# Gate and up products of two feed-forward layers: high weights times both halves of the activations in one product of 512 columns

## The chip, the cores and the metric

The program runs on one core of a Trainium2 chip. A core has TensorE (matrix products, with a queue of weight loads of its own), VectorE, ScalarE, GpSimd, SyncE (which here only starts transfers) and 16 DMA engines. The metric is the device time of one execution in microseconds, lower is better; the figure quoted for a kernel is the median of its runs.

## The reference, cut to what matters

The reference is a model of two blocks on 256 tokens of 1024 features. The first block has two layers, and each ends with a gated feed-forward. The change concerns the first two products of it, `h @ w1` (gate) and `h @ w3` (up):

```
D_FF = 2816
def swiglu(h, w1, w3, w2):
    return (jax.nn.silu(h @ w1) * (h @ w3)) @ w2

for i in range(2):                                    # the first block
    ...                                               # mixer: attention and convolution, or a Fourier transform
    x = x + g2 * swiglu(rmsnorm(x, norm2_g[i]) * (1 + sc2) + sh2, ffn_w1[i], ffn_w3[i], ffn_w2[i])
x = second_block(x, ...)                              # attention, recurrence, 32 experts, a last norm
```

The scales `sc2`, shifts and gates of a layer come from a product of a condition vector with a large matrix (`ada_w`), which the kernel computes alongside on VectorE.

## The kernel before, in words

The work is written out by hand for each engine: every engine runs its own list in order, and semaphores tie the lists together. Nothing schedules it at build time.

**High and low parts.** TensorE multiplies in a float32 form that keeps fewer bits. To keep float32 accuracy every operand is split: `wh` is the rounded weight tile and `wl` is what is left, `ah` and `al` are the same for the activations. A product is then three matmuls into one sum: `wh*ah`, `wh*al` and `wl*ah`. ScalarE makes the high part (a copy that rounds), VectorE the low part (a subtraction).

**A feed-forward layer** (`ffn(l)`, l = 0 or 1, one in each layer) walks over 22 tiles f of 128 hidden features. For each tile:
- TensorE `gate_up(f)`: for gate and for up (`half`), 8 steps j over the 1024 input features, three matmuls of 256 columns (the tokens) each: 48 matmuls, lines 808 to 810. Gate and up of one tile share one PSUM bank, `ps[f % 2]`.
- ScalarE `sigmoid(f)` reads gate (line 1338), then `ffn_hi` makes the high part of the gate and up weights of tile f + 2 (line 1317, 2048 columns), `mul_hi` the high part of the hidden tile (line 1342), `down_hi` that of the down weights of tile f + 1 (line 1348).
- VectorE `mul(f)`: gate times sigmoid (line 1910), times up (line 1912). `mul_lo` makes the low part of the hidden tile (line 1917), `wide_lo` that of the gate and up weights of tile f + 2 (line 1740, two instructions), `down_lo` that of the down weights of tile f + 1 (line 1922). Two `ada_step` instructions per tile (lines 1624 and 1625, 1024 columns) sum the product of the condition vector; each waits for a transfer into `araw`.
- TensorE `down(f)`: 24 matmuls of 256 columns, lines 821 to 823, once `mul_lo(f)` and `down_lo(f)` are there.

TensorE's order is gate_up(0), gate_up(1), down(0), then gate_up(f + 2), down(f + 1) and so on, so that VectorE and ScalarE have the time of the next gate_up to finish a tile. Tiles 0 to 19 run in a loop of five rounds of four tiles (`u` = 0 to 3), tiles 20 and 21 after it. SyncE starts, per tile, one transfer of 1 MB (gate and up weights), one of 0.5 MB (down weights) and two of 0.5 MB for `araw`; each waits until the tile that it overwrites has been used.

**After the last tile** VectorE does two ada steps (`ada(base_n + 42)` and `+ 43`), which release SyncE to fetch the last block of weights that ScalarE has to split (line 1175) before it squares x for the next norm (line 1185); TensorE sums the squares (line 611).

Of the kernel before, what the change touches and what calls it, by code (L numbers as in the profile page):

```python
# [15 lines left out]
P = 128  # L16
# [117 lines left out]
def build(nc, xT_d, xc_d, vec_d, con_d, cone_d, tab_d, ada_d, blk_d, uq_d, uk_d, ffna_d, ffnb_d, rga_d, rgx_d, rout_d,  # L134
# [5 lines left out]
    with ctx:  # L140
        def sb(name, shape, dt=F32, stack=ctx):
            return stack.enter_context(nc.sbuf_tensor(name, shape, dt))
# [33 lines left out]
        def q_scale(i):  # L176
# [8 lines left out]
        wl = sb("wl", [P, 6144], F32R, early)  # L185
        ah = sb("ah", [P, DJ * 2 * T], F32R, early)
        al = sb("al", [P, DJ * 2 * T], F32R, early)
        cone = sb("cone", [P, NE_], F32, early)
        ah3 = ah[:, :].rearrange("p (j t) -> p j t", j=DJ)
        al3 = al[:, :].rearrange("p (j t) -> p j t", j=DJ)  # L190
        ph = ExitStack()
# [144 lines left out]
        s_lg, s_tk, s_tke, s_mask, s_cum, s_route, s_ht, s_htok, s_flag = [sem(n) for n in (  # L336
            "logits", "top_values", "top_exp", "chosen", "slot_counts", "routed", "h_turned", "h_tokens", "overflow_known")]
        s_order, s_pick, s_gpp, s_gpc = [sem(n) for n in ("experts_ranked", "ranks_set", "places_product", "places_copied")]
# [8 lines left out]
        s_last = sem("last_output_copied")  # L347
        s_ot, s_fy = sem("out_turned"), sem("final_chunk")

# [208 lines left out]
        def _(pe):  # L558
# [239 lines left out]
            def ffn(l):  # L798
                def gate_up(f, fv, fresh=None):
                    wait(pe, s_flo, f + (l * NF + 1))  # L800
                    wait(pe, s_fm, f + (l * NF - 1))
                    for half in range(2):
                        for j in range(DJ):
                            if fresh is not None:
                                pe.wait_ge(s_hl, DJ * fresh + j + 1)
                            w0 = (fv % 2) * FA + half * D + j * P
                            o = ps[fv % 2][:, half * T:(half + 1) * T]
                            mm(o, wh[:, w0:w0 + P], ah3[:, j, 0:T], start=(j == 0), stop=False)  # L808
                            mm(o, wh[:, w0:w0 + P], al3[:, j, 0:T], start=False, stop=False)  # L809
                            last = mm(o, wl[:, w0:w0 + P], ah3[:, j, 0:T], start=False, stop=(j == DJ - 1))  # L810
                    last.then_inc(s_fgu, 1)
# [344 lines left out]
            for j in range(DJ):  # L1156
                mm(out_tile(j), ymo[:, j * P:(j + 1) * P], stt[:, (NU - 1) % 3, :], start=False, stop=True,
                   skip_group_check=True).then_inc(s_ot, 1)
            norm_sums(6)
# [3 lines left out]
        def _(act):  # L1163
# [171 lines left out]
            def ffn(l):  # L1335
                def sigmoid(f, slot):
                    wait(act, s_fgu, f + (l * NF + 1))
                    A(sg[:, slot, :], ps[slot][:, 0:T], ACT.Sigmoid).then_inc(s_fsig, 1)

# [270 lines left out]
        def _(dve):  # L1610
# [294 lines left out]
            def ffn(l, g_gate):  # L1905
                base_n, base_g = 48 + 48 * l, 6 + 6 * l

                def mul(f, slot):
                    wait(dve, s_fsig, f + (l * NF + 1))
                    TTn(sg[:, slot, :], ps[slot][:, 0:T], sg[:, slot, :], ALU.mult).then_inc(s_ft, 1)  # L1910
                    wait(dve, s_ft, f + (l * NF + 1))
                    TTn(mm_[:, slot, :], ps[slot][:, T:2 * T], sg[:, slot, :], ALU.mult).then_inc(s_fm, 1)

# [12 lines left out]
                with dve.Fori(0, (NF - 2) // 4) as i:  # L1926
# [4 lines left out]
                    for u in range(4):  # L1931
                        mul(f0 + u, u % 2)
                        for j in (2 * u, 2 * u + 1):
                            dve.wait_ge(s_araw[j % 2], loaded + 16 * (j // 2))
                            if j > 0:
                                dve.wait_ge(s_ada, n0 + j)
                            ada_step(accl[:, bass.ds(g0, AG)], araw[:, j % 2, :], csil[:, j:j + 1] if l == 0 else V("c2", j), j
                                     ).then_inc(s_ada, 1)
                            if j % 2 == 0:
                                mul_lo(f0 + u, u % 2)  # L1940
                                wide_lo(l, f0 + (2 + u), u)
                        down_lo(f0 + (u + 1), (u + 1) % 2)
# [451 lines left out]
```

## Time and profile before

| | us |
|---|---|
| median of 3 runs (1874.78, 1878.18, 1877.59) | 1877.59 |
| the profiled execution, whole | 1875.9 |
| its span, first to last instruction | 1874.1 |
| TensorE busy in the span | 1682.5 (90%) |
| VectorE busy | 808.7 (43%) |
| ScalarE busy | 436.9 (23%) |

The two feed-forward stages lie at about 270 to 462 us and 548 to 741 us of the span. After 1000 us the experts run. A row of the profile names the line of the kernel, the engine, the operation, and `out<-in` by the program's names. Shares over the whole span say little about a stage, since the stages have different limits.

### The profile page before, as it was taken

To read this page: it belongs to the slowest core of one execution; us is meant where nothing else is said; L and a number is where in the kernel's file an instruction comes from. 1 tells how busy PE (TensorE), PEld (TensorE's weight loads), DVE (VectorE), ACT (ScalarE), POOL (GpSimd) and SP (SyncE) were. 2 spreads that over 40 slices of the span, in tenths; PEclk is the share of its full clock that TensorE was granted. 3 is DMA by queue.
4 is the path that set the end of the run, shared out by engine and by line. 5 is a ranking of instruction groups with operands and counts; after the bars stand their busy time and mean duration, and the time that the engine had idled before them with its cause. 6 is when DMAs were issued, how large, how long until landed. Compare 5 with 4: busy or idle time off the path is not lost.

```text
span 1874.1 us, 24283 instructions
## 1 busy us (share of the span) xinstructions
PE 1682.5 (90%) x9444; PEld 1066.2 (57%) x9444; DVE 808.7 (43%) x1263; ACT 436.9 (23%) x679; POOL 157.1 (8%) x75
## 2 busy tenths in 40 slices
PE   5989799999899998876899999999987988799875
PEld 2863489998589998866633444334322433344222
DVE  5766568877348877575322222212211212122021
ACT  3324644443334443354200000000000000000001
POOL 1632010000210001452000000000000000000000
PEclk8998899999899999798899999999998999899988
DMA  8723448886328886334799999999999999999994
GB/s 323 248 79 142 150 157 304 305 302 240 144 102 305 310 298 230 130 146 150 300 392 421 421 421 422 421 421 421 421 422 421 421 422 422 420 410 422 421 421 196
DMA packets 100606, 586.61 MB, mean 313 GB/s; under 512 B 12224, under 2 KB 13504, under 8 KB 45152
## 3 DMA queue, kind: packets, MB, share of 16 engines
q1 hardware_dynamic: 100512, 585.35, 79.8%
q8 instruction: 59, 0.97, 0.2%
q14 instruction: 35, 0.29, 0.0%
HBM read 584.26 MB, written 1.05 MB: 312 GB/s over the span
## 4 chain that ended last, share of the span: by engine, by line
PE 74%; DMA 11%; DVE 8%; SPq 3%; ACT 2%; issue 1%; POOL 0%; DVEq 0%; ACTq 0%
PE psum L1047 22%; PE psum L1063 10%; PE psum L808 5%; PE psum L809 5%; PE psum L810 5%; DMA mraw<-dn_dram 5%; SPq L401 3%; PE psum L1023 3%; DMA mraw<-gu_dram 2%; PE psum L626 2%; PE psum L1076 2%; PE psum L627 2%; PE psum L628 2%; PE psum L823 2%; PE psum L822 2%; PE psum L821 2%
## 5 line engine op out<-in xcount | busy, mean ns | idle before, releaser
L1047 PE MATMUL psum<-mraw,xsat 128*64 128x512 f32 (+2 forms) x1648 | 416.5, 646 | 38.3 <-DMA mraw<-gu_dram 25.2
L1047 PEld LDWEIGHTS psum<-mraw,xsat 128*64 128x64 f32 (+2 forms) x1648 | 137.7, 144 | 272.4 <-issue 271.4
L1063 PE MATMUL psum<-mraw,xsat 128*64 128x512 f32 (+2 forms) x848 | 204.6, 620 | 13.4 <-DMA mraw<-dn_dram 10.7
L808 PE MATMUL psum<-ah,wh 128*128 128x256 f32 x704 | 202.5, 288 | 7.2 <-DVE al L1684 7.1
L1569 POOL TENSOR_TENSOR wl<-raw,wh 128x1024 fp32r<-128x1024 f32 x56 | 147.2, 2647 | 719.2 <-ACT wh L1175 689.9
L809 PE MATMUL psum<-al,wh 128*128 128x256 f32 x704 | 200.8, 285 | 0.0
L810 PE MATMUL psum<-ah,wl 128*128 128x256 f32 x704 | 200.7, 285 | 0.0
L626 PE MATMUL psum<-ah,wh 128*128 128x256 f32 (+1 forms) x440 | 136.1, 309 | 29.5 <-DVE al L2104 8.4
L1047 PE MATMUL psum<-mlast,xsat 128*64 128x512 f32 (+2 forms) x400 | 145.6, 648 | 17.0 <-DMA mraw<-gu_dram 17.0
L808 PEld LDWEIGHTS psum<-ah,wh 128*128 128x128 f32 x704 | 136.5, 194 | 8.5 <-issue 7.6
L1063 PEld LDWEIGHTS psum<-mraw,xsat 128*64 128x64 f32 (+2 forms) x848 | 68.0, 140 | 122.2 <-issue 120.3
L809 PEld LDWEIGHTS psum<-al,wh 128*128 128x128 f32 x704 | 136.9, 194 | 0.0
L810 PEld LDWEIGHTS psum<-ah,wl 128*128 128x128 f32 x704 | 136.8, 194 | 0.0
L2212 DVE TENSOR_TENSOR oacc<-psum,oacc 128x512 f32<-128x512 f32 x60 | 38.6, 686 | 220.9 <-PE psum L1076 220.9
L627 PE MATMUL psum<-al,wh 128*128 128x256 f32 (+1 forms) x440 | 132.6, 301 | 0.0
L628 PE MATMUL psum<-ah,wl 128*128 128x256 f32 (+1 forms) x440 | 132.3, 301 | 0.0
L1535 ACT ACTIVATE xsat<-psum 128x512 f32<-128x512 f32 x16 | 9.6, 599 | 436.2 <-PE psum L1096 436.2
L626 PEld LDWEIGHTS psum<-ah,wh 128*128 128x128 f32 x440 | 90.1, 205 | 36.1 <-issue 14.3
L1740 DVE TENSOR_TENSOR wl<-raw,wh 128x1024 fp32r<-128x1024 f32 x88 | 103.7, 1220 | 0.0
L821 PE MATMUL psum<-mh,wh 128*128 128x256 f32 x352 | 99.6, 283 | 0.0
L822 PE MATMUL psum<-ml,wh 128*128 128x256 f32 x352 | 99.6, 283 | 0.0
L823 PE MATMUL psum<-mh,wl 128*128 128x256 f32 x352 | 99.6, 283 | 0.0
(355 smaller groups left out, 2382.9 us busy)
## 6 DMA issues: line engine op xcount, KB each, us to landing
mraw<-gu_dram SPq DMA_DIRECT2D x206, 1024.0 KB, 19.8
mraw<-dn_dram SPq DMA_DIRECT2D x106, 1024.0 KB, 25.3
araw<-ada_dram SPq DMA_DIRECT2D x128, 512.0 KB, 4.7
mlast<-gu_dram SPq DMA_DIRECT2D x50, 1024.0 KB, 20.9
raw<-ffa_dram SPq DMA_DIRECT2D x44, 1024.0 KB, 7.7
raw<-blk_dram SPq DMA_DIRECT2D x56, 512.0 KB, 4.3
raw<-ffb_dram SPq DMA_DIRECT2D x44, 512.0 KB, 5.8
mlast<-dn_dram SPq DMA_DIRECT2D x22, 1024.0 KB, 26.1
```

Of the source, the lines that this page charges most:

```text
L626: mm(o, wh[:, w], ah3[:, j, 0:width], start=(j == 0), stop=False)
L627: mm(o, wh[:, w], al3[:, j, 0:width], start=False, stop=False)
L628: last = mm(o, wl[:, w], ah3[:, j, 0:width], start=False, stop=(j == DJ - 1))
L808: mm(o, wh[:, w0:w0 + P], ah3[:, j, 0:T], start=(j == 0), stop=False)
L809: mm(o, wh[:, w0:w0 + P], al3[:, j, 0:T], start=False, stop=False)
L810: last = mm(o, wl[:, w0:w0 + P], ah3[:, j, 0:T], start=False, stop=(j == DJ - 1))
L821: mm(o, wh[:, w0:w0 + P], a, start=first and j % 2 == 0, stop=False, skip_group_check=True)
L822: mm(o, wh[:, w0:w0 + P], b_, start=False, stop=False, skip_group_check=True)
L823: last = mm(o, wl[:, w0:w0 + P], a, start=False, stop=end, skip_group_check=True)
L1047: last = mm(ps[4 + n][a * w:(a + 1) * w, :], xs[:, k * P + a * w:k * P + (a + 1) * w], slots[slot][:, i * 2 * D + n * 512:i * 2 * D + (n + ...
L1063: last = mm(ps[n][a * w:(a + 1) * w, :], at[:, k * P + a * w:k * P + (a + 1) * w], slots[slot][:, i * D + n * 512:i * D + (n + 1) * 512], ...
L1569: sub = lambda o, a, b: nc.gpsimd.tensor_tensor(o, a, b.bitcast(F32), ALU.subtract)
```

## The change

Three things change together.

1. The two activation halves lie in one tensor, `ahl[:, 0]` high and `ahl[:, 1]` low. `gate_up` multiplies `wh` by both at once: one matmul of 512 columns fills a whole bank, columns 0 to 255 with `wh*ah`, columns 256 to 511 with `wh*al`. A second matmul of 256 columns adds `wl*ah` to the first half. Gate and up take a bank each, so four banks are used in place of two.
2. The two halves of a bank have to be added. ScalarE copies the right halves of gate and up to SBUF (into `rt` and `rstd`, which are free here), VectorE adds them to the left halves in PSUM (`halves`), and only then ScalarE takes the sigmoid.
3. VectorE's order within a tile changes: `halves`, the first ada step, `mul`, `wide_lo`, the second ada step, `mul_lo`, `down_lo`. Before it was `mul`, the first ada step, `mul_lo`, `wide_lo`, the second ada step, `down_lo`.

TensorE also waits for `s_mod` before gate_up(1), since bank 2 held a result of the condition vector's product; and one semaphore of the last stage is merged into another.

```diff
@@ gate_up, TensorE
-                            o = ps[fv % 2][:, half * T:(half + 1) * T]
-                            mm(o, wh[:, w0:w0 + P], ah3[:, j, 0:T], start=(j == 0), stop=False)
-                            mm(o, wh[:, w0:w0 + P], al3[:, j, 0:T], start=False, stop=False)
-                            last = mm(o, wl[:, w0:w0 + P], ah3[:, j, 0:T], start=False, stop=(j == DJ - 1))
+                            bank = ps[2 * (fv % 2) + half]
+                            if j < DJ - 1:
+                                mm(bank[:, :], wh[:, w0:w0 + P], ahl4[:, :, j, 0:T], start=(j == 0), stop=False)
+                                mm(bank[:, 0:T], wl[:, w0:w0 + P], ah3[:, j, 0:T], start=False, stop=False)
+                            else:
+                                mm(bank[:, 0:T], wl[:, w0:w0 + P], ah3[:, j, 0:T], start=False, stop=False)
+                                last = mm(bank[:, :], wh[:, w0:w0 + P], ahl4[:, :, j, 0:T], start=False, stop=True)
@@ ffn, TensorE
                 gate_up(0, 0, fresh=1 + l)
+                pe.wait_ge(s_mod, 6 + 6 * l)
                 gate_up(1, 1)
@@ sigmoid, ScalarE
                     wait(act, s_fgu, f + (l * NF + 1))
-                    A(sg[:, slot, :], ps[slot][:, 0:T], ACT.Sigmoid).then_inc(s_fsig, 1)
+                    A(rt[:, T:2 * T], ps[2 * slot][:, T:2 * T], ACT.Copy)
+                    A(rstd[:, T:2 * T], ps[2 * slot + 1][:, T:2 * T], ACT.Copy).then_inc(s_fsig, 1)
+                    wait(act, s_fsum, f + (l * NF + 1))
+                    A(sg[:, slot, :], ps[2 * slot][:, 0:T], ACT.Sigmoid).then_inc(s_fsig, 1)
@@ ffn, VectorE
+                def halves(f, slot):
+                    wait(dve, s_fsig, f * 2 + (l * NF * 2 + 1))
+                    gate, up = ps[2 * slot][:, 0:T], ps[2 * slot + 1][:, 0:T]
+                    TTn(gate, gate, rt[:, T:2 * T], ALU.add).then_inc(s_fsum, 1)
+                    TTn(up, up, rstd[:, T:2 * T], ALU.add)
...
                     for u in range(4):
-                        mul(f0 + u, u % 2)
+                        halves(f0 + u, u % 2)
                         for j in (2 * u, 2 * u + 1):
...
                             if j % 2 == 0:
+                                mul(f0 + u, u % 2)
+                                wide_lo(l, f0 + (2 + u), u)
+                            else:
                                 mul_lo(f0 + u, u % 2)
-                                wide_lo(l, f0 + (2 + u), u)
                         down_lo(f0 + (u + 1), (u + 1) % 2)
+                halves(NF - 2, 0)
                 mul(NF - 2, 0)
...
+                halves(NF - 1, 1)
                 mul(NF - 1, 1)
```

On VectorE, the first tile of a round of the loop (u = 0). Before; `accl` is the sum of the condition vector's product, `wl` from `raw,wh` a low part of weights, `ml` the low part of the hidden tile:

```order
L1910 TENSOR_TENSOR sg<-psum,sg 128x256 [waits ffn_sigmoid]
L1912 TENSOR_TENSOR mm_<-psum,sg 128x256 [waits ffn_gate]
...
L1624 TENSOR_SCALAR accl<-araw,csil 128x1024
L1917 TENSOR_TENSOR ml<-mm_,mh 128x256 [waits ffn_mul_hi]
...
L1740 TENSOR_TENSOR wl<-raw,wh 128x1024 [waits ffn_hi]
L1740 TENSOR_TENSOR wl<-raw,wh 128x1024
...
L1922 TENSOR_TENSOR wl<-raw,wh 128x1024 [waits ffn_down_hi]
```

The same place on VectorE with the change (its own line numbers):

```order
L1924 TENSOR_TENSOR psum<-psum,rt 128x256 [waits ffn_sigmoid]
L1925 TENSOR_TENSOR psum<-psum,rstd 128x256
...
L1631 TENSOR_SCALAR accl<-araw,csil 128x1024
...
L1917 TENSOR_TENSOR sg<-psum,sg 128x256 [waits ffn_sigmoid]
...
L1919 TENSOR_TENSOR mm_<-psum,sg 128x256 [waits ffn_gate]
...
L1747 TENSOR_TENSOR wl<-raw,wh 128x1024 [waits ffn_hi]
L1747 TENSOR_TENSOR wl<-raw,wh 128x1024
...
L1632 SCALAR_TENSOR_TENSOR accl<-araw,csil,accl 128x1024 [waits ada_acc]
L1930 TENSOR_TENSOR ml<-mm_,mh 128x256 [waits ffn_mul_hi]
...
L1935 TENSOR_TENSOR wl<-raw,wh 128x1024 [waits ffn_down_hi]
```

The two additions come first, and the row that writes `ml` has moved from behind the first ada step to behind `wide_lo` and the second ada step.

On ScalarE, the head of a round of the loop. Before:

```order
L1338 ACT_TABLE_LOAD
L1338 ACTIVATE sg<-psum 128x256 [waits ffn_gate_up]
L1315 ISA
L1317 ACTIVATE wh<-raw 128x2048 [waits wide_loaded0]
L1342 ACTIVATE mh<-mm_ 128x256 [waits ffn_mul]
```

And with the change:

```order
L1342 ACT_TABLE_LOAD
L1342 ACTIVATE rt<-psum 128x256 [waits ffn_gate_up]
L1343 ACTIVATE rstd<-psum 128x256
L1345 ACT_TABLE_LOAD
L1345 ACTIVATE sg<-psum 128x256 [waits ffn_halves_added]
L1319 ISA
L1321 ACTIVATE wh<-raw 128x2048 [waits wide_loaded0]
L1349 ACTIVATE mh<-mm_ 128x256 [waits ffn_mul]
```

Two copies stand ahead of the sigmoid, and a second load of ScalarE's function table now stands between them and the sigmoid. It does so only here, once a round; the other three tiles of a round and tiles 20 and 21 have none.

## Rows read from the trace of the kernel before

**Rows 1.** By window: us, busy PE, PEld, DVE, ACT, POOL; clock; DMA share, GB/s.

```profile
275.00:460.00 185.00, 185.00 (x1544) 185.00 (x1544) 146.30 (x172) 80.58 (x91) 0.76 (x1) 1.00 0.83 289
```

**Rows 2.** Timeline, TensorE, gate_up: start us, length us, engine, line.

```profile
350.06 0.28 PE L808 MATMUL psum<-ah,wh 128*128 128x256 f32 x1
...
355.46 0.28 PE L808 MATMUL psum<-ah,wh 128*128 128x256 f32 x1
```

**Rows 3.** Timeline, TensorE, products of 512 columns in the first stage.

```profile
64.07 0.40 PE L626 MATMUL psum<-ah,wh 128*128 128x512 f32 x1
...
73.60 0.39 PE L626 MATMUL psum<-ah,wh 128*128 128x512 f32 x1
```

**Rows 4.** Timeline, VectorE, one tile of feed-forward 0 and the next one's start.

```profile
353.19 0.42 DVE L1910 TENSOR_TENSOR sg<-psum,sg 128x256 f32<-128x256 f32 x1 [1.51 <-ACT sg L1338]
...
354.00 1.27 DVE L1625 SCALAR_TENSOR_TENSOR accl<-araw,csil,accl 128x1024 f32 x1
355.30 0.42 DVE L1917 TENSOR_TENSOR ml<-mm_,mh 128x256 fp32r<-128x256 f32 x1
355.64 2.36 DVE L1740 TENSOR_TENSOR wl<-raw,wh 128x1024 fp32r<-128x1024 f32 x2
357.91 1.28 DVE L1625 SCALAR_TENSOR_TENSOR accl<-araw,csil,accl 128x1024 f32 x1
359.11 1.22 DVE L1922 TENSOR_TENSOR wl<-raw,wh 128x1024 fp32r<-128x1024 f32 x1
361.83 0.42 DVE L1910 TENSOR_TENSOR sg<-psum,sg 128x256 f32<-128x256 f32 x1 [1.51 <-ACT sg L1338]
```

**Rows 5.** Timeline, ScalarE, the same tile.

```profile
352.78 0.38 ACT L1338 ACTIVATE sg<-psum 128x256 f32<-128x256 f32 x1 [4.64 <-PE psum L810]
353.06 1.90 ACT L1317 ACTIVATE wh<-raw 128x2048 fp32r<-128x2048 f32 x1
```

**Rows 6.** Timeline, ScalarE, tiles 0 and 1 of feed-forward 0.

```profile
274.58 1.28 ACT L1338 ACT_TABLE_LOAD   x1
277.90 0.38 ACT L1338 ACTIVATE sg<-psum 128x256 f32<-128x256 f32 x1 [2.03 <-PE psum L810]
...
283.66 0.39 ACT L1338 ACTIVATE sg<-psum 128x256 f32<-128x256 f32 x1 [2.32 <-PE psum L810]
```

**Rows 7.** Timeline, VectorE, tiles 0 to 2 of feed-forward 0.

```profile
279.11 0.74 DVE L1624 TENSOR_SCALAR accl<-araw,csil 128x1024 f32 x1
280.42 0.42 DVE L1917 TENSOR_TENSOR ml<-mm_,mh 128x256 fp32r<-128x256 f32 x1 [0.56 <-ACT mh L1342]
...
285.36 0.42 DVE L1910 TENSOR_TENSOR sg<-psum,sg 128x256 f32<-128x256 f32 x1
...
295.56 1.29 DVE L1625 SCALAR_TENSOR_TENSOR accl<-araw,csil,accl 128x1024 f32 x1 [1.96 <-DMA araw<-ada_dram]
```

**Rows 8.** Timeline, TensorE, idle gaps of 1.6 to 3 us.

```profile
269.65 0.36 PE L808 MATMUL psum<-ah,wh 128*128 128x256 f32 x1 [2.55 <-DVE al L1684]
...
844.89 0.66 PE L915 MATMUL psum<-con,p 128*128 128x128 f32 x4 [2.20 <-DVE p L2047]
...
853.67 3.41 PE L946 MATMUL psum<-q,con 128*128 128x256 f32 x8 [2.22 <-ACT q L1463]
```

**Rows 9.** TensorE in the 4 us behind three such gaps: us, busy, clock.

```profile
270.00:274.00 4.00, 3.89 (x18) 0.57 0.00 0
845.00:849.00 4.00, 2.27 (x13) 1.00 0.00 0
854.00:858.00 4.00, 4.00 (x12) 0.57 0.00 0
```

**Rows 10.** Chain of waits, end of feed-forward 0: start us, length us, what.

```profile
456.46 0.39 ACT sg L1338
...
459.97 3.25 DVE acc L1625
...
463.67 4.94 DMA raw<-blk_dram
```

More of the change, by code:

```diff
@@ L185, in build @@
         wl = sb("wl", [P, 6144], F32R, early)
-        ah = sb("ah", [P, DJ * 2 * T], F32R, early)
-        al = sb("al", [P, DJ * 2 * T], F32R, early)
+        ahl = sb("ahl", [P, 2, DJ * 2 * T], F32R, early)
         cone = sb("cone", [P, NE_], F32, early)
-        ah3 = ah[:, :].rearrange("p (j t) -> p j t", j=DJ)
-        al3 = al[:, :].rearrange("p (j t) -> p j t", j=DJ)
+        ahl4 = ahl[:, :, :].rearrange("p a (j t) -> p a j t", j=DJ)
+        ah3, al3 = ahl4[:, 0], ahl4[:, 1]
         ph = ExitStack()
@@ L329, in build @@
         s_th, s_lruo = sem("lru_tanh"), sem("lru_out")
+        s_fsum = sem("ffn_halves_added")
         s_zero = sem("pads_cleared")
@@ L336, in build @@
         s_lg, s_tk, s_tke, s_mask, s_cum, s_route, s_ht, s_htok, s_flag = [sem(n) for n in (
-            "logits", "top_values", "top_exp", "chosen", "slot_counts", "routed", "h_turned", "h_tokens", "overflow_known")]
+            "logits", "top_values", "top_exp", "chosen", "slot_counts", "routed", "tokens_and_output_turned", "h_tokens", "overflow_known")]
         s_order, s_pick, s_gpp, s_gpc = [sem(n) for n in ("experts_ranked", "ranks_set", "places_product", "places_copied")]
@@ L347, in build @@
         s_last = sem("last_output_copied")
-        s_ot, s_fy = sem("out_turned"), sem("final_chunk")
+        s_fy = sem("final_chunk")
         def out_tile(j):
@@ L1157, in _ @@
                 mm(out_tile(j), ymo[:, j * P:(j + 1) * P], stt[:, (NU - 1) % 3, :], start=False, stop=True,
-                   skip_group_check=True).then_inc(s_ot, 1)
+                   skip_group_check=True).then_inc(s_ht, 1)
             norm_sums(6)
@@ L1908, in mul @@
                 def mul(f, slot):
-                    wait(dve, s_fsig, f + (l * NF + 1))
-                    TTn(sg[:, slot, :], ps[slot][:, 0:T], sg[:, slot, :], ALU.mult).then_inc(s_ft, 1)
+                    wait(dve, s_fsig, f * 2 + (l * NF * 2 + 2))
+                    TTn(sg[:, slot, :], ps[2 * slot][:, 0:T], sg[:, slot, :], ALU.mult).then_inc(s_ft, 1)
                     wait(dve, s_ft, f + (l * NF + 1))
-                    TTn(mm_[:, slot, :], ps[slot][:, T:2 * T], sg[:, slot, :], ALU.mult).then_inc(s_fm, 1)
+                    TTn(mm_[:, slot, :], ps[2 * slot + 1][:, 0:T], sg[:, slot, :], ALU.mult).then_inc(s_fm, 1)
+                def halves(f, slot):
[3 more added lines that the diff above has]
+                    TTn(up, up, rstd[:, T:2 * T], ALU.add)
                 def mul_lo(f, slot):
@@ L2271, in _ @@
             for j in range(DJ):
-                dve.wait_ge(s_ot, j + 1)
+                dve.wait_ge(s_ht, 4 + j + 1)
                 STT(x[:, j, :], out_tile(j), m_col(17, j), x[:, j, :], ALU.mult, ALU.add).then_inc(s_x, 1)
```

## The prediction

> **What bounds the kernel now.** I read the busy times by window first, since the change touches two stages only. Over 275 to 460 us, feed-forward 0, TensorE is busy for all of the 185.00 us at a granted clock of 1.00 (2.4 GHz); VectorE works 146.30 us of it and the DMA engines 83% [rows 1]. So TensorE sets the pace of the stage, and I read the timelines of the engines next, to see how much room the others have. The second layer looks alike.
>
> TensorE's pace: from the L808 row at 350.06 to the one at 355.46 there are 45 matmuls, so one of 256 columns takes 0.120 us [rows 2]. A tile has 48 in gate_up and 24 in down, 72 x 0.120 = 8.64 us, which is just the distance of the two L1910 rows, 353.19 and 361.83 [rows 4]. In each tile VectorE sits idle for 1.51 us before L1910, waiting for ScalarE's sigmoid, and ScalarE 4.64 us for TensorE [rows 4, 5]. At the ends of a stage another thing decides, the chain of waits [rows 10], which I come to below.
>
> **TensorE, the gain.** The columns do not change: 512 + 256 is 3 x 256. What goes is one matmul and one weight load out of three. How much is that? In the first stage the kernel has products of 512 columns: from 64.07 to 73.60 there are 42 of them, 0.227 us each [rows 3], where two of 256 take 0.240 us. The saving is 0.013 us per pair, 16 pairs per tile, 0.21 us, and gate_up falls from 5.76 to 5.55 us, the tile from 8.64 to 8.43. The first gate_up of a stage is fed by VectorE and partly at the low clock, so I count half of it, 0.1. Two stages: 2 x (21 x 0.21 + 0.1) = 9.0 us, if every tile stays at TensorE's pace.
>
> The Trainium skill, "TensorE: Matmul & The Clock Gate", section "Wait — 56ns, not 53.3ns?", gives a fixed cost of about 2.5 ns per matmul at the high clock; by that, 704 matmuls fewer would save 1.8 us, not 9.0, and the change would come out 7 us later. The trace disagrees: 0.120 us is 13 ns over 256 columns at 2.4 GHz, and the wide rows carry the same 13 ns once [rows 2, 3].
>
> **VectorE and ScalarE in an ordinary tile.** Let z be the moment when ScalarE starts on a tile. Before, the copy from PSUM takes 0.28 us to the next start and 0.38 to its end, the copy of 2048 columns 1.90, and VectorE starts at z + 0.41 [rows 4, 5]. VectorE's pieces from start to start: two multiplications 0.81, first ada step 1.30, `mul_lo` 0.34, `wide_lo` 2.27, ada step 1.20, `down_lo` about 1.2 [rows 4]. With the change: copies to 0.66; additions from 0.69 to 1.39 (I take 0.35 each, a row of the same kind and size; no row shows VectorE writing PSUM); ada step to 2.6; sigmoid done at 1.5, hidden; `mul` to 3.4; the wide copy of ScalarE is done at 3.3, hidden; `wide_lo` to 5.7; ada step to 6.9; `mul_lo` done at 7.3; `down_lo` to 8.4. TensorE wants `mul_lo` at z + 8.43 (down of the tile before, 2.88, and a gate_up, 5.55), and VectorE is wanted again at 8.43 + 0.69 = 9.12. Both are met: margins 1.1 and 0.7 us. Bounds of an addition: 0.28 (ScalarE's copy of the size) to 0.74 (a 1024-column step of VectorE, the next dearer row [rows 7]). At the upper end two additions cost 0.8 us more and eat the margins without passing them by more than 0.1.
>
> In a tile with u = 0, the order of ScalarE now has a table load of 1.28 us [rows 6] between the copies and the sigmoid. Copies to 0.66, load to 1.96, sigmoid to 2.36, wide copy 2.26 to 4.16. VectorE's ada step is the short one here (0.74, [rows 7]), but `wide_lo` has to wait until 4.18; it ends at 6.45, the ada step at 7.65, `mul_lo` at 8.07. TensorE wants it at 8.43. Hidden, with a margin of only 0.36.
>
> **The start of a stage, a new stall.** TensorE's order there is gate_up(0), gate_up(1), down(0): only one gate_up lies between the end of tile 0's gate_up and its down, not a down and a gate_up. So TensorE wants `mul_lo(0)` at z + 5.55. Before, that row began at 280.42, z being 277.90: z + 2.5, early by 3 us [rows 6, 7]. Now it is a tile with u = 0, done at 8.09 as above. TensorE stands still for 8.09 - 5.55 = 2.54 us, in each of the two stages: 5.1 us. Nothing behind it on TensorE's queue can fill in.
>
> A second stall follows in tile 2. VectorE left tile 0 at 285.36, z + 7.46, and now leaves at z + 9.14, and `down_lo(1)` releases SyncE, behind which the loads of tile 4 and of `araw` queue. The ada step of tile 2 already waited 1.96 us for its transfer, until z + 17.66 [rows 7]. I move the landing by the same 1.7 to 19.3; this step now stands ahead of `mul`, so `mul_lo(2)` follows 5.9 us later (1.2 + 0.8 + 2.3 + 1.2 + 0.4), at 25.2. TensorE wants it at 8.09 + 2.88 + 5.55 + 8.43 = 24.95. Cost 0.3 us, in feed-forward 0. Together 5.4.
>
> **The end of a stage, a longer chain.** The chain that ends the stage goes from the last gate_up through ScalarE's sigmoid at 456.46, VectorE, an ada step of 3.25 us (slowed beside GpSimd), then SyncE and a transfer of 4.94 us that ScalarE must split before the next norm [rows 10]. Tile 21 has no table load, but the chain gets longer: the multiplication began 0.41 after z; now copies 0.66, addition 0.42, sigmoid 0.39 and three hand-overs of 0.03 make 1.57. That is 1.16 per stage, 2.3 us. TensorE's down(21) also waits 0.4, but this lies beside the chain.
>
> Sum without the clock: -9.0 + 5.4 + 2.3 = -1.3 us. The profiled execution took 1875.9 (span 1874.1 and 1.8 around it), 1.7 below the median; applied to the median, 1877.6 - 1.3 = 1876.3.
>
> **The clock.** The new stall is a gap of 2.5 us in the middle of dense work. What did such gaps do? After 2.55 us before 269.65 the granted clock was 0.57 over the next 4 us, that is, it fell to 1.2 GHz for most of them, which cost 0.43 x 4 = 1.7 us. After 2.22 us before 853.67 it was 0.57 too. After 2.20 us before 844.89 it stayed at 1.00 [rows 8, 9]. So a fall is likelier than not. During it TensorE is slower, VectorE catches up, and the second stall of 0.3 goes. With a fall in both stages: -1.3 + 3.4 - 0.3 = +1.8, and 1877.6 + 1.8 = 1879.4; with one, about 1877.9. The wait on `s_mod` costs nothing: it is released at the stage's start, beside gate_up(0). I predict 1879.0.
>
> **The rivals.**
> - *Only the gain comes* (16%): start and end do not cost, because VectorE gets through tile 0 before TensorE needs it, or the transfer behind the chain lands when it did. For it: TensorE sets the pace over 185 us. Against it: the order of `mul_lo` behind `wide_lo`. Time 1877.6 - 9.0 = 1868.6; with half of the cost 1872.
> - *The wide product saves nothing* (12%, slower): its moving operand is in two pieces 16 KB apart, and no row shows such a one at 512 columns. If the step from one piece to the next costs the 13 ns that a matmul's start costs, the gain is nil, and stalls, chain and clock stay: +5.4 + 2.3 + 1 to 3 = about 1887. It decides from 8 ns per product on. (The 2.5 ns of the Trainium skill, "TensorE: Matmul & The Clock Gate", would put the time near here as well, at 1886; rows 2 and 3 leave it hardly a chance.)
> - *The low clock lasts longer* (13%, slower): over 6 to 7 us per gap, 3.3 us each: 1876.3 + 6.6 = 1882.9.
> - *VectorE becomes the pace* (5%, slower): its tile has 7.0 us beside the two additions, so it passes TensorE's 8.43 from 0.72 us per addition on and the old 8.64 from 0.82 on. At 1.0 us it would be 9.0 us per tile, 38 x 0.36 = +14, and 1893.
>
> **How the numbers follow.** The forecast (clock falls once or twice) has 54%, own range 1875 to 1882. What can be told from no change is 0.2%, 3.8 us: 1873.8 to 1881.4. Faster: the first rival and a little of the forecast's lower side, 18%. Slower: the last three rivals, all but a few parts of the long fall, 28%. Within: 54%. The range reaches from the first rival's edge to the unsaving product, 1869 to 1887.
>
> **What would show it.** Right: L809 and L813 of 512 columns 0.227 us apart from the next start; tiles 8.43 us apart; TensorE idle about 2.5 us before the first down row of each stage, waiting for VectorE's `ml`; `mul_lo` 8.1 us after z in tile 0; a second table load between copy and sigmoid in ten tiles; the granted clock at 0.5 behind the gap; the ada steps of tile 21 about 1.2 us later after z. Wrong: tiles at 8.64 or more, or idle time of TensorE in the middle of a stage (the margins were too thin); no gap at the start (then faster by 5); additions over 0.7 us.

## The result, and the profile after

The changed kernel takes 1879.08 us (median of 20 runs, 1873.79 to 1886.41), the kernel before 1874.80 in the runs beside it (20 runs, 1871.31 to 1878.18). The ratio is 1.0022 with a 95% interval of 1.0013 to 1.0031: 4.1 us slower, 2.4 to 5.8. The profiled execution took 1873.79 us, span 1872.0, the shortest of its 20; so I compare stretches of the two traces, not their spans.

The window of [rows 1], and behind it the 4 us after the new gap in feed-forward 0 and in feed-forward 1 (columns as there):

```profile
275.00:460.00 185.00, 182.15 (x1187) 166.06 (x1185) 158.47 (x212) 99.38 (x139) 0.00 (x0) 0.99 0.82 289
286.00:290.00 4.00, 4.00 (x22) 3.96 (x21) 3.97 (x8) 2.81 (x4) 0.00 (x0) 0.57 0.83 278
566.00:570.00 4.00, 4.00 (x27) 3.58 (x27) 3.97 (x6) 2.88 (x3) 0.00 (x0) 1.00 0.80 284
```

TensorE, busy without a break before, now stands idle for 2.85 us of the 185; VectorE works 12.2 us more and ScalarE 18.8. The granted clock is at its lower level (1.2 GHz) for most of the 4 us behind the first gap (0.57) and not behind the second (1.00). Both gaps are in TensorE's timeline, each ahead of the first `down` of its stage:

```profile
285.09 0.36 PE L824 MATMUL psum<-mh,wh 128*128 128x256 f32 x1 [2.63 <-DVE ml L1930]
...
563.95 0.36 PE L824 MATMUL psum<-mh,wh 128*128 128x256 f32 x1 [2.63 <-DVE ml L1930]
```

What TensorE waits for is VectorE's row L1930. VectorE in tile 0 of feed-forward 0, answering to [rows 7]:

```profile
277.55 0.43 DVE L1924 TENSOR_TENSOR psum<-psum,rt 128x256 f32<-128x256 f32 x1 [2.62 <-ACT rstd L1343]
277.89 0.42 DVE L1925 TENSOR_TENSOR psum<-psum,rstd 128x256 f32<-128x256 f32 x1
278.23 0.75 DVE L1631 TENSOR_SCALAR accl<-araw,csil 128x1024 f32 x1
279.25 0.42 DVE L1917 TENSOR_TENSOR sg<-psum,sg 128x256 f32<-128x256 f32 x1 [0.28 <-ACT sg L1345]
279.70 0.42 DVE L1919 TENSOR_TENSOR mm_<-psum,sg 128x256 f32<-128x256 f32 x1
281.05 2.36 DVE L1747 TENSOR_TENSOR wl<-raw,wh 128x1024 fp32r<-128x1024 f32 x2 [0.92 <-ACT wh L1321]
283.33 1.28 DVE L1632 SCALAR_TENSOR_TENSOR accl<-araw,csil,accl 128x1024 f32 x1
284.52 0.42 DVE L1930 TENSOR_TENSOR ml<-mm_,mh 128x256 fp32r<-128x256 f32 x1
```

And ScalarE beside it, answering to [rows 6]:

```profile
276.86 0.38 ACT L1342 ACTIVATE rt<-psum 128x256 f32<-128x256 f32 x1 [1.89 <-PE psum L813]
277.14 0.38 ACT L1343 ACTIVATE rstd<-psum 128x256 f32<-128x256 f32 x1
277.54 1.28 ACT L1345 ACT_TABLE_LOAD   x1
278.83 0.38 ACT L1345 ACTIVATE sg<-psum 128x256 f32<-128x256 f32 x1
...
282.49 0.38 ACT L1342 ACTIVATE rt<-psum 128x256 f32<-128x256 f32 x1 [0.22 <-PE psum L813]
```

z is 276.86. The second table load is there, 1.28 us between copies and sigmoid; `mul_lo` is done at 284.94, z + 8.08; the next tile's gate_up took 282.49 - 276.86 = 5.63 us. So the stall is 8.08 - 5.63 = 2.45 us and the hand-overs. The wait for `s_mod` costs nothing: gate_up(1) shows no idle time of TensorE ahead of it or in it.

The second stall that was forecast for tile 2 does not follow, but small ones do in mid-stage. The dearest in feed-forward 0 is in tile 10, on VectorE and then on TensorE:

```profile
365.91 1.28 DVE L1632 SCALAR_TENSOR_TENSOR accl<-araw,csil,accl 128x1024 f32 x1 [1.08 <-DMA araw<-ada_dram]
...
371.36 0.42 DVE L1930 TENSOR_TENSOR ml<-mm_,mh 128x256 fp32r<-128x256 f32 x1
```

```profile
371.42 0.40 PE L813 MATMUL psum<-ahl,wh 128*128 128x512 f32 x1
371.93 0.36 PE L824 MATMUL psum<-mh,wh 128*128 128x256 f32 x1
```

The ada step ahead of `mul` waits 1.08 us for its transfer, `mul_lo` is done at 371.78, and TensorE starts `down` 0.51 us behind the last wide product, where 0.23 us is usual. ScalarE's starts on a tile lie 8.48 us apart in most tiles, 8.83 there, and 8.51 in most where TensorE takes up a tile with a table load (u = 0). Over the 19 tile distances behind the gap this adds up to 0.6 us in feed-forward 0 and, with 8.77 once (a wait of 1.01 us for `araw`), 0.5 us in feed-forward 1.

TensorE in gate_up (answers to [rows 2, 3]):

```profile
307.93 0.40 PE L809 MATMUL psum<-ahl,wh 128*128 128x512 f32 x1
308.17 0.28 PE L810 MATMUL psum<-ahl,wl 128*128 128x256 f32 x1
...
308.64 0.40 PE L809 MATMUL psum<-ahl,wh 128*128 128x512 f32 x1
```

From 307.93 to 308.64 lie two pairs of a wide and a narrow product. Between 304 and 330 us the wide product has a mean of 0.234 us to the next start and the narrow one behind it 0.117; by the distance of the tiles, (8.48 - 24 x 0.120) / 16, a pair takes 0.350 us. I had 0.347.

The chain of waits at the end of feed-forward 0 (answers to [rows 10]):

```profile
457.08 0.38 ACT rt L1342
457.46 0.28 ACT rstd L1343
457.77 0.44 DVE psum L1924
458.24 0.39 ACT sg L1345
458.65 0.44 DVE sg L1917
...
461.75 3.24 DVE acc L1632
...
465.44 5.04 DMA raw<-blk_dram
```

From ScalarE's start on tile 21 to the multiplication it is now 458.65 - 457.08 = 1.57 us. Behind it every step is as long as before within 0.1 us.

The measure that the experiments share is the length of a stage: from the first matmul of gate_up(0) to the first L611 (norm sums) behind the stage.

| kernel | feed-forward 0 | feed-forward 1 |
|---|---|---|
| before | 269.65 to 472.51: 202.9 | 547.93 to 750.36: 202.4 |
| changed | 268.76 to 474.38: 205.6 | 547.05 to 750.39: 203.3 |

These lengths are read from one profiled execution of each kernel. What lies behind the two stages differs between such executions by more than most edits are worth: from the norm sums behind feed-forward 1 to those of the next norm it is 142.8 us in the kernel before, 141.6 in the changed one, 146.2 in e2 and 145.9 in e6, with the granted clock at its lower level for longer in the latter two.

### The profile page after: what moved, and what is told of

It reads as the page before. It is cut to its first block, busy times and chain, and to the rows that moved or that the text cites. A ratio compares the mean times of both kernels' runs of the same rounds, so it can differ in the third digit from the quotient of the medians.

```text
span 1872.0 us, 23142 instructions
## 1 busy us (share of the span) xinstructions
PE 1673.5 (89%) x8740; PEld 1024.4 (55%) x8740; DVE 838.7 (45%) x1351; ACT 477.9 (26%) x777; POOL 157.3 (8%) x75
## 4 chain that ended last, share of the span: by engine, by line
PE 74%; DMA 9%; DVE 9%; SPq 4%; ACT 2%; issue 2%; POOL 0%; DVEq 0%; ACTq 0%
PE psum L1051 21%; PE psum L1067 10%; PE psum L809 8%; SPq L401 4%; PE psum L810 4%; PE psum L1027 3%; DMA mraw<-dn_dram 3%; DMA mraw<-gu_dram 3%; PE psum L1080 2%; PE psum L626 2%; PE psum L824 2%; PE psum L627 2%; PE psum L628 2%; PE psum L825 2%; PE psum L826 2%
## 5 line engine op out<-in xcount | busy, mean ns | idle before, releaser
L809 PE MATMUL psum<-ahl,wh 128*128 128x512 f32 x616 | 224.7, 402 | 7.1 <-DVE ahl L1691 7.1
L1067 PE MATMUL psum<-mraw,xsat 128*64 128x512 f32 (+2 forms) x848 | 205.2, 622 | 12.1 <-DMA mraw<-dn_dram 9.7
L810 PE MATMUL psum<-ahl,wl 128*128 128x256 f32 x616 | 174.2, 283 | 0.0
L626 PE MATMUL psum<-ahl,wh 128*128 128x256 f32 (+1 forms) x440 | 135.6, 308 | 29.7 <-DVE ahl L2121 8.4
L809 PEld LDWEIGHTS psum<-ahl,wh 128*128 128x128 f32 x616 | 117.0, 190 | 33.9 <-issue 7.5
L627 PE MATMUL psum<-ahl,wh 128*128 128x256 f32 (+1 forms) x440 | 132.1, 300 | 0.0
L628 PE MATMUL psum<-ahl,wl 128*128 128x256 f32 (+1 forms) x440 | 131.8, 299 | 0.0
L810 PEld LDWEIGHTS psum<-ahl,wl 128*128 128x128 f32 x616 | 118.0, 192 | 2.2
L626 PEld LDWEIGHTS psum<-ahl,wh 128*128 128x128 f32 x440 | 89.5, 203 | 37.2 <-issue 13.3
L2241 DVE COPY ymo<-psum 128x512 f32<-128x512 f32 x15 | 10.4, 692 | 193.9 <-PE psum L1067 193.9
L627 PEld LDWEIGHTS psum<-ahl,wh 128*128 128x128 f32 x440 | 89.9, 204 | 1.2 <-issue 0.2
```

What stands on the lines that cost most here:

```text
L626: mm(o, wh[:, w], ah3[:, j, 0:width], start=(j == 0), stop=False)
L627: mm(o, wh[:, w], al3[:, j, 0:width], start=False, stop=False)
L628: last = mm(o, wl[:, w], ah3[:, j, 0:width], start=False, stop=(j == DJ - 1))
L809: mm(bank[:, :], wh[:, w0:w0 + P], ahl4[:, :, j, 0:T], start=(j == 0), stop=False)
L810: mm(bank[:, 0:T], wl[:, w0:w0 + P], ah3[:, j, 0:T], start=False, stop=False)
L1067: last = mm(ps[n][a * w:(a + 1) * w, :], at[:, k * P + a * w:k * P + (a + 1) * w], slots[slot][:, i * D + n * 512:i * D + (n + 1) * 512], ...
```

## The experiments

Each ratio is to the kernel before on the same chip. Its median was 1876.27 us beside the first four kernels, 1875.28 beside the next four and 1875.17 beside the last.

**e1: the wide products alone.** TensorE's part of the change on the kernel before (the diff shows what else follows from it). It leaves out the product of the high weights with the low activations (it stands in the upper half of the bank, and nothing adds it), and with it copies and additions.

```diff
-A(sg[:, slot, :], ps[slot][:, 0:T], ACT.Sigmoid).then_inc(s_fsig, 1)
+A(sg[:, slot, :], ps[2 * slot][:, 0:T], ACT.Sigmoid).then_inc(s_fsig, 1)    # at once: no copy, no sum
...
-TTn(mm_[:, slot, :], ps[slot][:, T:2 * T], sg[:, slot, :], ALU.mult).then_inc(s_fm, 1)
+TTn(mm_[:, slot, :], ps[2 * slot + 1][:, 0:T], sg[:, slot, :], ALU.mult).then_inc(s_fm, 1)
```

> The kernel before with only TensorE's part of the change: wide products into four banks, and neither the copies nor the additions (the product of high weights and low activations is left out of gate and up). Theory A (the gain is real but mis-sized: a pair of products takes 0.350 us, not 0.347): tiles 8.48 us apart, no new gap at the start of a stage, nothing longer at its end, 21 x 0.16 + 0.1 per stage, together 7 us faster than before, ratio 0.9963. With the size of the prediction, 0.21 per tile, 9 us faster, 0.9952. Rival (the wide product saves nothing by itself): 1.000.

Measured: 1869.39 us, ratio 0.9964 [0.9951, 0.9977]. The stages take 199.5 (270.40 to 469.90) and 199.1 us, 3.4 and 3.3 less than before. That is the gain by itself: 6.7 to 6.8 us, not 9.0. The pair costs 0.350 here too, with no copies and additions beside it.

**e2: the low part at once.** `mul_lo` right behind `mul`.

```diff
 mul(f0 + u, u % 2)
+mul_lo(f0 + u, u % 2)
 wide_lo(l, f0 + (2 + u), u)
```

> The change with the low part of the hidden tile put back ahead of wide_lo, right behind the two multiplications. Theory A (the gap at the start comes from the order on VectorE): mul_lo of tile 0 is done 4.9 us after ScalarE starts on the tile, ahead of the 5.6 at which TensorE wants it, so the gap of 2.6 us in each stage goes, and the fall of the clock behind it; ends stay 1.16 us longer per stage. 5.2 for the gaps and 1.7 to 3.4 for the clock less than with the change: 3 to 4 us faster than before, ratio 0.998. Rival (the gaps are covered elsewhere, the loss is contention over a whole stage): as with the change, 1.002.

Measured: 1884.34, ratio 1.0046 [1.0034, 1.0059], slower than the change itself. The gap at the start did go: a low part that was early enough is enough for that. But in VectorE's timeline, two tiles:

```profile
312.87 0.42 DVE L1924 TENSOR_TENSOR psum<-psum,rt 128x256 f32<-128x256 f32 x1
...
315.85 0.43 DVE L1930 TENSOR_TENSOR ml<-mm_,mh 128x256 fp32r<-128x256 f32 x1 [0.78 <-ACT mh L1349]
...
320.79 0.42 DVE L1924 TENSOR_TENSOR psum<-psum,rt 128x256 f32<-128x256 f32 x1
...
322.66 1.28 DVE L1632 SCALAR_TENSOR_TENSOR accl<-araw,csil,accl 128x1024 f32 x1 [1.11 <-DMA araw<-ada_dram]
...
325.22 0.42 DVE L1930 TENSOR_TENSOR ml<-mm_,mh 128x256 fp32r<-128x256 f32 x1 [0.48 <-ACT mh L1349]
```

It waits in every tile for ScalarE's `mh` (0.5 to 0.8 us, 1.2 in tile 0) and in about every second one for `araw`. A tile has 8.4 us, VectorE's work in it 7.7, so such waits fit once, not twice. In most tiles L1924 has no idle time ahead of it any more: VectorE is the pace. By window, TensorE in e2 and in the changed kernel:

```profile
340.00:380.00 40.00, 38.91 (x253) 34.91 (x253) 34.38 (x46) 22.82 (x30) 0.00 (x0) 1.00 0.85 298
```

```profile
340.00:380.00 40.00, 39.88 (x260) 36.09 (x259) 35.92 (x48) 23.14 (x30) 0.00 (x0) 1.00 0.86 306
```

At the end of the stage VectorE is behind by 2.0 us, and TensorE waits there (1.99 before 461.80) for what it no longer waits for at the start. The stages take 206.5 and 205.2 us, 0.9 and 1.9 more than the changed kernel's. This is my fourth rival, made by an edit that was to help.

**e3: the table once.** The sigmoid's table at the head of ScalarE's loop, ahead of the copies.

```diff
 r0 = act.snap(i * 32)
+load_table(ACT.Sigmoid)
 for u in range(4):
```

> The change with a one-element sigmoid at the head of each round of ScalarE's loop, so that the table is loaded there once, while ScalarE waits for TensorE, and none lies between copies and sigmoid. Theory A: in tile 0 wide_lo starts 0.9 us earlier, at 3.3 us after ScalarE's start, mul_lo is done at 7.2 in place of 8.1; the gap shrinks from 2.6 to 1.6 us, and tiles in mid-stage do not change. 2 us less than with the change, ratio to before 1.001. Rival (the second load costs nothing, the ada step covers it): 1.002.

Measured: 1877.16, ratio 1.0013 [1.0002, 1.0024]. The gaps are 1.82 us each, for the 1.6 expected; the clock stays at 1.00 behind both. The stages take 204.4 and 202.4 us, 1.2 and 0.9 less than the changed kernel's. They are for theory A; the interval of the time holds 1.001 and 1.002 alike. Contrary to what was expected, tiles in mid-stage change too: they are 8.48 us apart throughout, without the small stalls of the changed kernel.

**e4: the operand in one piece.** Both halves of the activations side by side, so that the 512 columns are contiguous.

```diff
-ahl = sb("ahl", [P, 2, DJ * 2 * T], F32R, early)
+ahl = sb("ahl", [P, DJ, 2, 2, T], F32R, early)
```

> The change with high and low activations of a step side by side, so that the 512 columns of the moving operand are one piece. If the two pieces are why a wide product takes 0.233 to 0.236 us and not the 0.227 of the first stage: 0.227 here, tiles 8.43 apart, 2 us less than with the change, ratio to before 1.001; the products of 512 columns in the first stage, now in two pieces, get slower by as much. If it is what runs beside TensorE (the reads of the other engines, transfers): 0.235 here too, tiles 8.48 apart, 1.002.

Measured: 1880.13, ratio 1.0025 [1.0012, 1.0037]; wide products have a mean of 0.234 us. The products of the first stage, now in two pieces, keep their 0.227 (median). So the two pieces are not why the wide ones here are dearer than 0.227.

**e5: the last tile in the old form.** Three narrow products, no copies, no additions in tile 21.

```diff
+for u in range(4):                                 # last round, written out
+    gate_up(NF - 4 + u, u, narrow=(u == 3))
...
-halves(NF - 1, 1)
```

> The changed kernel, but the last tile (21) of each feed-forward is computed in the old form: three products of 256 columns, no copies, no additions (TensorE's last round of four tiles is written out behind its loop). Theory A, the longer chain at the end is paid in full: from ScalarE's start on tile 21 to the start of the multiplication 0.41 us instead of 1.57, so 1.16 us per stage less, and 0.16 us more for the narrow products: 2.0 us less than the changed kernel, ratio to before 1.0011. Rival, the transfer of blocks behind the ada step lands when it did, so the chain is hidden: 1.0022 to 1.0024.

Measured: 1876.92, ratio 1.0009 [0.9997, 1.0021]. Feed-forward 1 takes 202.4 us (549.32 to 751.71), 0.9 less than the changed kernel's; feed-forward 0 takes 205.6 as before, with the clock low for longer after its start (0.50 in 274 to 278, where the changed kernel has 1.00). The time agrees with theory A, but its interval ends only just below the rival's 1.0022; what speaks clearly is feed-forward 1, where 1.16 - 0.16 = 1.0 us was expected.

**e6: the low part one step earlier.**

```diff
 wide_lo(l, f0 + (2 + u), u)
+mul_lo(f0 + u, u % 2)
...
-    mul_lo(f0 + u, u % 2)      # behind the second ada step
```

> The changed kernel, but in every tile of the loop VectorE takes the low part of the multiplied tile (mul_lo) right behind wide_lo, ahead of the second ada step, not behind it. Theory A (the order of mul_lo is what stops TensorE at the start, and the wait for ScalarE's copy is what made it dear right behind mul): ready 1.2 us earlier in tile 0, the gap of 2.63 us becomes 1.4, no wait for ScalarE's mh (ready at z + 3.8, VectorE there at z + 5.7), 2.4 us less, ratio 1.0009. Rival B, every other order of VectorE costs what it brings, because each ada step that starts later holds back its transfer: 1.002 to 1.0045, with VectorE waiting for araw in most rounds.

Measured: 1880.31, ratio 1.0018 [1.0003, 1.0032]. The timeline shows a gap of 1.43 us in feed-forward 0 and 1.47 in feed-forward 1, as expected:

```profile
287.08 0.36 PE L824 MATMUL psum<-mh,wh 128*128 128x256 f32 x1 [1.43 <-DVE ml L1930]
```

The clock stayed at 1.00 behind both. Feed-forward 1 is 1.4 us shorter than the changed kernel's (201.9), as theory A has it. Feed-forward 0 is not (205.5): in the profiled execution the transfer that ends it took 6.41 us for 5.04, and the low clock that it was spared behind the gap it had longer at the start (until 278.13, 8.0 us behind the stage's start; 3.7 us in the changed kernel). So the time of this one kernel tells A and B hardly apart; e7 does.

**e7: the three together** (e3, e5, e6).

> The changed kernel with the last tile in the old form, mul_lo right behind wide_lo, and the sigmoid table loaded at the head of ScalarE's loop. Theory A: the gain of the wide products alone was 6.8 us (0.9964); what is left against it is a gap of 0.6 us per stage (2.63 - 1.2 - 0.8) and 0.16 us for each narrow tile: 6.8 - 1.2 - 0.3 = 5.3 us, 0.9972 if the clock does not fall behind so short a gap, 0.999 if it falls in each stage. Rival B (the order costs elsewhere): no faster than 1.000.

Measured: 1870.21, ratio 0.9981 [0.9967, 0.9995], faster than before by 3.6 us. The stages take 200.4 (268.28 to 468.65) and 200.5 (543.23 to 743.72), together 4.4 us less than before, the gaps are 0.63 us:

```profile
282.80 0.36 PE L829 MATMUL psum<-mh,wh 128*128 128x256 f32 x1 [0.63 <-DVE ml L1942]
```

The clock stays at 1.00 behind them. Theory A, with 5.3 us expected and 3.6 (0.9 to 6.2) measured; rival B, no faster than 1.000, lies outside the interval.

**e8: wide and narrow products in groups.** 7 wide, 8 narrow, 1 wide in each half.

```diff
+for j in range(DJ - 1): mm(bank[:, :], wh..., ahl4[:, :, j, 0:T], start=(j == 0), stop=False)
+for j in range(DJ):     mm(bank[:, 0:T], wl..., ah3[:, j, 0:T], start=False, stop=False)
+last = mm(bank[:, :], wh..., ahl4[:, :, DJ - 1, 0:T], start=False, stop=True)
```

> The changed kernel, but TensorE's order in a half of gate_up is 7 products of 512 columns, 8 of 256, one of 512, not one of 512 and one of 256 in turn (first tile of a stage as it was). Theory A, the change of width makes a wide product 0.233 us instead of 0.227 and the narrow one behind it 0.1164 instead of 0.120: grouped they are 0.227 and 0.120, pair 0.347 for 0.350, 2 us less, ratio 1.0011. Rival B, what runs beside (weights written, DMA, VectorE and ScalarE on PSUM) makes the wide one 0.233: it stays, the narrow one is 0.120, pair 0.353, 2 us more, 1.0033.

Measured: 1878.64, ratio 1.0026 [1.0013, 1.0038]. TensorE's timeline, one half of gate_up and the next one's start:

```profile
308.25 1.77 PE L808 MATMUL psum<-ahl,wh 128*128 128x512 f32 x7
309.86 1.11 PE L811 MATMUL psum<-ahl,wl 128*128 128x256 f32 x8
310.81 0.40 PE L813 MATMUL psum<-ahl,wh 128*128 128x512 f32 x1
311.05 1.77 PE L808 MATMUL psum<-ahl,wh 128*128 128x512 f32 x7
```

Seven wide ones take 1.61 us, 0.230 each; eight narrow ones 0.95, 0.119 each; the half 2.80, 0.350 a pair as before. Both theories are wrong: the order moves 4 ns from one product to the other and the sum stays. The time, 1.0026, lies between the two and excludes only theory A's 1.0011. Why the pair needs 0.350, not 0.347, remains open.

**e9 and e10: the block that ends the stage, loaded earlier.** In the chain of all kernels so far the transfer `raw<-blk` comes last, because SyncE has it queued behind ada loads that wait for VectorE's steps after the last tile. One move on SyncE's queue, in the kernel before (e9) and in the changed one (e10):

```diff
-for j in range(6):
+for j in range(4):
     ada(base_n + 40 + j)
 sp.wait_ge(s_fblo, (l + 1) * NF)
 blk(shared)
+for j in range(4, 6):
+    ada(base_n + 40 + j)
```

> The kernel before, with one move on SyncE's queue: the load of the block that ends the chain (raw<-blk) is issued ahead of the ada loads 44 and 45, not behind them. The two ada loads wait for VectorE's steps behind the last tile, so the block was issued at 463.67 and landed at 468.6; now it waits only for down_lo(21) and is there before TensorE's last product. Theory A (this transfer ends both stages): what is left is TensorE's last down, at about 461, VectorE's x, free of its ada step at 463.2 and eight rows later at 466.3, or ScalarE's split and table load, at about 464: 4 to 6 us less per stage, ratio 0.994 to 0.997. Rival B (x or the ada steps end the stage anyway, or the stage behind waits for loads that are issued later): 0.999 to 1.001.

> The changed kernel with the same move on SyncE's queue and nothing else. Theory A: the additions' 1.16 us stands ahead of VectorE's ada steps and x, so that it is still paid, and the change still costs what it did: ratio to the run before with the block early the same 1.002 as without, 0.996 to 0.999 to the kernel before. Rival B (the transfer made the longer chain visible, and without it the last down of TensorE ends the stage): 1.16 us per stage less between the two, ratio between them 1.001.

Measured: e9 1862.58, ratio 0.9936 [0.9920, 0.9953]; e10 1864.52, ratio 0.9943 [0.9930, 0.9957]. Stages of e9: 196.4 (273.62 to 470.02) and 196.7 (542.61 to 739.30), 6.5 and 5.7 us less than before. So the transfer did end them. VectorE, ScalarE and TensorE at the end of feed-forward 0 in e9:

```profile
462.95 4.62 DVE L1627 SCALAR_TENSOR_TENSOR acc<-araw,csil,acc 128x1024 f32<-128x1024 f32 x2
467.50 3.21 DVE L1956 SCALAR_TENSOR_TENSOR x<-psum,mod,x 128x256 f32<-128x256 f32 x8
```

```profile
465.57 2.01 ACT L1177 ACTIVATE wh<-raw 128x1024 fp32r<-128x1024 f32 x2 [2.05 <-DMA raw<-blk_dram]
467.60 1.28 ACT L1181 ACT_TABLE_LOAD   x1
```

```profile
466.26 0.28 PE L825 MATMUL psum<-mh,wl 128*128 128x256 f32 x1
466.47 3.62 PE L596 MATMUL psum<-accl,cone 128*32 128x512 f32 x20
470.02 3.72 PE L613 MATMUL psum<-work,con 128*128 128x256 f32 x16
```

TensorE now goes without idle time from its last `down` (row at 466.26) through 20 products for the condition vector (L596) to the norm sums (L613, in the kernel before L611). So by the measure of the stages its own list ends them, in both stages. ScalarE, which still waited 2.05 us for the block, squares x from 469.00, behind its table load, and the first row of x was done at 467.92. The chain of waits, which follows what ends last behind the stage, runs through VectorE: ada steps, the rows of x, two more ada steps and the reciprocal of the norm.

The stages of e10 (199.4 and 197.4) stand to those of e9 as the changed kernel's do to those of before: 3.0 and 0.7 us longer, for 2.8 and 0.9. The additions are still paid, but by another way than theory A has it: TensorE's last `down` waits for `mul_lo(21)`, and its last row starts 6.34 us after z in e10 and 5.44 in e9, 0.9 us later. Part of the 3.0 is the clock behind the gap (see below). The two ratios are 0.0007 apart with intervals of 0.0015 to either side and decide nothing.

**e11 and e12: everything together.** e11 is e7 with the block early. e12 has VectorE's ada step 43 behind the rows of x:

```diff
-for j in range(2, 4):
-    ada(base_n + 40 + j)
+ada(base_n + 42)
 dve.wait_ge(s_fdn, 1 + (l + 1) * NF)
 for j in range(DJ): ...                           # rows of x
-for j in range(4, 6):
+for j in range(3, 6):
```

> The kernel of three edits (last tile narrow, mul_lo right behind wide_lo, table at the loop's head; 0.9981) with the block's load early as well. If the gains add up: 0.9981 less the 4 to 6 us per stage of the block, 0.992 to 0.995. If the block's transfer was not what held the stage: 0.998.

> The same, and VectorE takes ada step 43 (3.25 us beside GpSimd) behind the eight rows of x, not ahead of them. If x then ends the stage: x starts 1.3 us earlier (TensorE's last down at 458.2 for 459.6), another 1 to 1.3 us per stage, ratio 0.001 below the one without. If ScalarE's split and table load end it: the same ratio within 0.0003.

Measured: e11 1856.06, ratio 0.9893 [0.9877, 0.9909], the fastest kernel here; e12 1860.79, ratio 0.9921 [0.9907, 0.9934]. e11's stages take 194.6 (269.32 to 463.96) and 194.5 (535.11 to 729.59), together 16.2 us less than before, where the time is 20 less (17 to 23). The rest lies between the two stages, 71.2 us from the first norm sum to the start of feed-forward 1 for 75.4 before. TensorE in the norm sums behind feed-forward 0, before and in e11:

```profile
472.51 6.72 PE L611 MATMUL psum<-work,con 128*128 128x256 f32 x16 [6.78 <-ACT work L1185]
```

```profile
463.96 3.72 PE L613 MATMUL psum<-work,con 128*128 128x256 f32 x16 [0.72 <-ACT work L1199]
```

The same 16 products took 3.0 us more where 6.78 us of idle time stood ahead of them: the granted clock was 0.55 over those 6.72 us, and 1.00 over the 3.72 us in e11.

For e12 the second theory holds for the stages: they are about as long (195.1 and 194.7), and in feed-forward 0 TensorE waits 0.82 us for ScalarE, which squares x directly behind its table load. The time is another matter, since what follows is later. VectorE behind feed-forward 1, in e12 and then in e11:

```profile
740.67 1.28 DVE L1646 SCALAR_TENSOR_TENSOR acc<-araw,vec,acc 128x1024 f32<-128x1024 f32 x1 [2.15 <-DMA araw<-ada_dram]
...
741.94 1.75 DVE L1695 RECIPROCAL rstd<-rt 128x256 f32<-128x256 f32 x1
```

```profile
730.25 3.96 DVE L1646 SCALAR_TENSOR_TENSOR acc<-araw,vec,acc 128x1024 f32<-128x1024 f32 x2
...
734.21 1.75 DVE L1695 RECIPROCAL rstd<-rt 128x256 f32<-128x256 f32 x1
```

The norm sums began at 734.84 and 729.59, so the reciprocal comes 7.1 us after them in e12 and 4.6 in e11. I read it so: three ada steps now stand between x and the reciprocal where e11 has two; the moved step releases its buffer later, the next load comes later, and the third step waits 2.15 us for it. Behind feed-forward 0 the same costs 1.3 us (norm sums to reciprocal 5.64 us for 4.34). Together this is 3.8 of the 4.7 us between the medians.

## Why the prediction was right, and where it was off

**The pace and the gain.** TensorE did stay the pace: tiles were 8.47 us apart (VectorE's L1924 at 304.55, 313.02 and 321.51). The mechanism of the gain was right and the size too large: the term of the sum that was mis-sized is the saving per pair, 0.013 us by [rows 3], which is a stream of wide products in another stage. It measured 0.010 (0.360 to 0.350), so 0.16 us per tile for 0.21, and 6.7 for 9.0 in all (e1), 2.3 us less.

**The tile of VectorE and ScalarE.** The additions take 0.42 us each and 0.34 from start to start, as taken; so the rival of VectorE as pace did not come by their price. The margin of a tile with a table load was mis-sized, though. `mul_lo` is done at z + 8.08, as forecast, but TensorE's `down` starts at z + 8.28 where nothing delays it (in tile 8, z being 346.38), not at 8.43: z is ScalarE's start, and by then TensorE has been at its next product for 0.20 us (380.48 and 380.68 in tile 12). With the hand-over of 0.15 us (284.94 to 285.09) some 0.05 us of the 0.36 is left. And the waits for `araw` ahead of `mul` (1.08 us in tile 10) were looked for in tile 2 alone. So "idle time of TensorE in the middle of a stage", a sign of being wrong, did come, at 0.6 and 0.5 us. With `mul_lo` earlier (e3, e6) it is gone. How near VectorE was to being the pace all the same, e2 shows: two waits of half a microsecond and more per tile bring it.

**The stall at the start.** 2.54 us forecast, 2.63 measured, in both stages, with the cause as named: e3 takes 0.81 off it, e6 1.2, both together 2.0. The second stall of 0.3 us, in tile 2, did not come: the clock fell behind the first gap of feed-forward 0, and with that the forecast let it go.

**The end.** 1.16 us forecast and measured (1.57 for 0.41). That it is paid in full is shown by e5 in feed-forward 1, in one execution.

**The clock.** Forecast: it falls behind one of the gaps or both, 1.7 us each. In the profiled executions of the five kernels with a gap of 2.6 to 2.7 us (the changed one, e4, e5, e8, e10) the granted clock was 0.57 to 0.69 over the 4 us behind it in feed-forward 0 each time, and stayed at 1.00 in feed-forward 1 each time. Behind gaps of 1.82 us and less (e3, e6, e7, e11, e12) it did not fall. So once, 0.43 x 4 = 1.7 us. What makes the two stages differ stays open; no run was made to find it. How often the clock falls in executions without a profile is not known either.

**The sum.** -6.7 + 2 x 2.63 + 2 x 1.16 + 1.7 = +2.6 us, and the small stalls in mid-stage add 0.6 + 0.5: +3.7, which is what the stages show (2.8 + 0.9). The times show +4.1 [2.4, 5.8]. The prediction gave +0.3 for one fall of the clock, 1.8 for two, and took 1.4 between them; one fall came. From its +0.3 to the +3.7 the terms that were off are the gain (2.3 us) and the stalls in mid-stage (1.1 us, put at nothing). The predicted 1879.0 met the 1879.08 by luck: the median of before turned out 2.8 us lower over more runs; the smaller gain and the small stalls came to 3.4 us more, and the second fall, of which 1.1 us had been counted, did not come.

**The rivals.** "Only the gain comes" and "VectorE becomes the pace" did not come; "the wide product saves nothing" was a quarter true. The Trainium skill, "TensorE: Matmul & The Clock Gate", section "Wait — 56ns, not 53.3ns?", gives about 2.5 ns of fixed cost per matmul at the high clock; these rows again show another figure, since one matmul less saves 10 ns here.

## What to carry to other kernels

Fewer, wider products pay at once on TensorE, but where they leave partial sums to other engines, look at the places where no slack has built up: the first tile of a stage (what is the engine's next demand, and what stands ahead of it on the queue of the supplier?) and the last. Treat those tiles apart, and let the wide form have the middle. And read the chain at the end of a stage to its last link: here a load queued behind two others that had to wait cost more (12 us by e9's ratio) than all the matmuls saved were worth.

When a new term lengthens a queue, redo the margin of every kind of tile from the rows of both engines, start of the one to start of the other; here 0.36 us on paper was 0.05.

A step moved on a queue also moves the release of its buffer, and so a later load (e2, e12); follow it to the next wait before you call the move free.

## What the runs showed of the hardware

- A product of 512 columns with weights of 128x128 takes 0.227 us in one stage [rows 3] and 0.234 on average in this one (0.230 in e8), the narrow one behind it 0.117 to 0.119 instead of 0.120. Neither a contiguous operand (e4), nor the missing copies and additions (e1), nor the order (e8) changed the pair's 0.350.
- VectorE adding from PSUM and SBUF into PSUM costs the same as writing SBUF: 0.42 us for 128x256, 0.34 to the next start.
- Behind the same gap of 2.6 to 2.7 us the granted clock came down in feed-forward 0 in five kernels of five and in feed-forward 1 in none (one profiled execution each).
- Idle time ahead of a short piece of work on TensorE cost twice here, by itself and by the low clock behind it: behind 6.78 us of it 16 products took 6.72 us, behind 0.72 us they took 3.72 (before at a granted clock of 0.55, e11 at 1.00).
- ScalarE's load of its function table takes 1.28 us, and the sigmoid follows at once (277.54 and 278.83 in the changed kernel).
